# Where the experts end in a two-block transformer kernel: the fold of the experts' sum moves into the last down part, VectorE's usual way past the overflow test stands first and takes the norm in, SyncE loads the next projection's first slots inside its own branch

## The reference, cut to what matters

```python
def _moe(h, w_router, w_gate, w_up, w_down):            # layer 1 of the first block
    ...
    for e in range(N_EXPERTS):
        out = out + gates[..., e:e + 1] * _swiglu(h, w_gate[e], w_up[e], w_down[e])
    return out
...
    x = x + g2 * y                                      # g2 is a row over the 1024 columns
...
def second_block(x, norm1_g, w_in, ...):
    h = rms_norm(x, norm1_g[l])
    proj = h @ w_in[l]                                  # z, xbc, dt, q, k, v, two gates
    ...
    xbc = silu(causal_dwconv(xbc, conv_w, conv_b))      # 4 taps along the tokens
```

## Time and profile before

| | |
|---|---|
| median of 3 runs | 2148.12 us |
| the 3 runs | 2144.53, 2148.12, 2155.45 us |
| span of the profiled execution | 2154.6 us, mean TensorE clock 0.951 |
| time of the profiled execution | not told apart from the three; the longest, 2155.45, is 0.8 above the span |
| TensorE busy | 2001.1 us, 93% |
| VectorE busy | 1670.7 us, 78% |
| ScalarE busy | 1329.6 us, 62% |
| experts' last us and border | about 1330 to 1440 us of the span |

### The profile page before, as it was taken

How to read it: one execution, slowest core, us unless ns; L and a number is a source line. 1 busy time by engine, 2 the same in 40 slices (tenths; PEclk the granted TensorE clock), 3 DMA queues, 4 the chain that set the end, 5 groups by cost and what they waited for, 6 DMA issues and landing times. The chain is left out here.

```text
span 2154.6 us, 27980 instructions
## 1 busy us (share of the span) xinstructions
PE 2001.1 (93%) x11071; PEld 1718.9 (80%) x11071; DVE 1670.7 (78%) x2154; ACT 1329.6 (62%) x1969; POOL 0.2 (0%) x4
## 2 busy tenths in 40 slices
PE   7878999987899999999999999979999988889999
PEld 4668778877778888888888887769877877878997
DVE  5877888676679989998998999778665755567884
ACT  2654443366578777787877776657556644545662
POOL 0000000000000000000000000000000000000000
PEclk8977999998899999999999999999999999889999
DMA  7625688731259989998999998745414532224553
GB/s 297 227 80 194 262 317 329 265 142 40 98 194 370 366 335 358 361 363 327 362 361 347 344 374 319 271 179 177 137 59 139 196 132 99 81 90 148 193 177 117
DMA packets 70377, 497.18 MB, mean 231 GB/s; under 512 B 8032, under 2 KB 8288, under 8 KB 10976
## 3 DMA queue, kind: packets, MB, share of 16 engines
q1 hardware_dynamic: 69952, 494.28, 62.4%
q10 hardware_dynamic: 288, 1.05, 0.1%
HBM read 494.25 MB, written 1.05 MB: 230 GB/s over the span
## 5 line engine op out<-in xcount | busy, mean ns | idle before, releaser
L338 DVE TENSOR_TENSOR wlo<-ring,whi 128x1024 fp32r<-128x1024 f32 (+1 forms) x845 | 1016.3, 1216 | 283.3 <-ACT whi L384 265.4
L384 ACT ACTIVATE whi<-ring 128x1024 fp32r<-128x1024 f32 (+1 forms) x845 | 886.1, 1054 | 494.7 <-PE ps L236 447.5
L236 PE MATMUL ps<-whi,hT 128*128 128x256 f32 (+2 forms) x944 | 323.3, 343 | 26.9 <-DVE hTl L292 7.0
L236 PE MATMUL ps<-wlo,hT 128*128 128x256 f32 (+2 forms) x944 | 317.6, 336 | 0.0
L236 PE MATMUL ps<-whi,hTl 128*128 128x256 f32 (+2 forms) x944 | 317.0, 336 | 0.0
L236 PE MATMUL ps<-whi,xg 128*128 128x512 f32 (+1 forms) x768 | 290.6, 378 | 5.4 <-DVE wlo L338 5.2
L236 PE MATMUL ps<-whi,xgl 128*128 128x512 f32 (+1 forms) x768 | 286.8, 373 | 0.0
L236 PE MATMUL ps<-wlo,xg 128*128 128x512 f32 (+1 forms) x768 | 286.4, 373 | 0.0
L236 PEld LDWEIGHTS ps<-whi,hT 128*128 128x128 f32 x944 | 185.5, 196 | 51.4 <-issue 7.1
L236 PE MATMUL ps<-whi,hf 128*128 128x512 f32 x528 | 209.5, 397 | 6.5 <-DVE wlo L338 4.7
L236 PE MATMUL ps<-wlo,hf 128*128 128x512 f32 x528 | 206.9, 392 | 0.0
(11 more groups left out here) (286 smaller groups left out, 2628.5 us busy)
## 6 DMA issues: line engine op xcount, KB each, us to landing
ring<-in_wstream SPq DMA_DIRECT2D x462, 1024.0 KB, 5.1
ring<-in_wstream SPq DMA_DIRECT2D x4, 832.0 KB, 5.3
ring<-in_wstream SPq DMA_DIRECT2D x6, 256.0 KB, 2.7
cst<-in_cst SPq DMA_DIRECT2D x1, 1028.0 KB, 7.5
x<-in_x SPq DMA_DIRECT2D x1, 1024.0 KB, 13.6
work<-in_bias ACTq DMA_DIRECT2D x2, 512.0 KB, 5.2
ring<-in_wstream SPq DMA_DIRECT2D x2, 512.0 KB, 3.8
out_x<-x SPq DMA_DIRECT2D x1, 512.0 KB, 2.8
```

The costliest lines, as they stand in the source:

```text
L236: i = self.e.matmul(out, lhsT, rhs, start=start, stop=stop, skip_group_check=True)
L338: i = self.e.tensor_tensor(K.wlo[:, q % NS, 0:cols], src, hi.bitcast(F32), ALU.subtract)
L384: i = self.e.activation(K.whi[:, q % NS, 0:cols], K.ring[:, m % RING, at:at + cols], ACT.Copy)
```

## The change

It has four parts. (1) `dve_fold` leaves group 3 of gate and up and stands in expert 7's down part, a quarter behind the low halves of parts 6, 8, 10 and 12; the overflow test follows two chunks later. (2) VectorE no longer uses `when_over` but `when_few`: the test is turned round, the usual way (128 or fewer) falls through, and the second pass is the `Else`. Both ways now hold the norm n1 as well, with chunks 0 and 1 of xbc ahead of its blocks; the usual way ends with a jump past the second pass. (3) ScalarE makes the high halves of chunks 0 and 1 among the squares, BETWEEN leaves chunks 2 and 3 (before blocks 4 and 6), and TensorE spreads the root after 8 of the 16 transposes instead of after all. (4) SyncE loads the first four slots of xbc inside its branch; on the usual way it waits for the ring slots as the eight experts leave them (`earlier`), and not for the step.

```diff
@@ -368,7 +368,7 @@
                 i = self.e.activation(out, a, fn, scale=scale, bias=bias, accum_out=accum)
             i.then_inc(self.done.sem, inc)
 
-    def split_to(self, n):
+    def split_to(self, n, fence=None):
 
         K = self.K
         while self.q < n:
@@ -378,7 +378,7 @@
             cols = blocks[0][2] * len(blocks)
             self.wait_ge(K.full[m % RING], 16 * (m // RING + 1))
             if q >= NS:
-                self.wait_ge(K.pe, ("w", q - NS))
+                self.wait_ge(K.pe, ("w", q - NS if fence is None else earlier(q, fence, NS)))
             inc = K.hi.up()
             if self.e is not None:
                 i = self.e.activation(K.whi[:, q % NS, 0:cols], K.ring[:, m % RING, at:at + cols], ACT.Copy)
@@ -395,14 +395,14 @@
         super().__init__(K, e, K.sp, K.full)
         self.m = 0
 
-    def load_to(self, n):
+    def load_to(self, n, fence=None):
 
         K = self.K
         while self.m < n:
             m = self.m
             self.m += 1
             if m >= RING:
-                self.wait_ge(*K.last_use[m - RING])
+                self.wait_ge(*K.last_use[m - RING if fence is None else earlier(m, fence, RING)])
             full = K.full[m % RING]
             inc = full.up(by=16)
             if self.e is not None:
@@ -411,6 +411,48 @@
                 off = K.off[index]
                 src = K.wstream[off * 128:(off + cols) * 128].rearrange("(p c) -> p c", p=128)
                 self.e.dma_start(K.ring[:, m % RING, 0:cols], src).then_inc(full.sem, inc)
+
+
+def earlier(m, fence, ring):
+
+    return fence - 1 - (fence - 1 - m) % ring
+
+
+def when_few(K, x, body, first, then):
+
+    if x.e is None:
+        q, held = x.q, dict(x.held)
+        first()
+        head = [s.n for s in x.own]
+        body()
+        K.over = (head, [s.n for s in x.own], x.q)
+        then(True)
+        x.held = held
+        return
+    head, tail, behind = K.over
+    q, held, had = x.q, dict(x.held), [s.n for s in x.own]
+    v = x.e.value_load(K.count[0:1, 8:9], min_val=0, max_val=256)
+    with x.e.If(v <= 128):
+        first()
+        assert head == [s.n for s in x.own]
+        for s, n, m in zip(x.own, head, tail):
+            x.e.wait_ge(s.sem, n)
+            x.e.sem_inc(s.sem, m - n)
+            s.n = m
+        x.q = behind
+        then(False)
+        after, ended = x.q, [s.n for s in x.own]
+    with x.e.Else():
+        K.again = True
+        for s, n in zip(x.own, had):
+            s.n = n
+        x.q, x.held = q, dict(held)
+        first()
+        body()
+        then(True)
+        assert x.q == after and ended == [s.n for s in x.own]
+        K.again = False
+    x.held = held
 
 
 def when_over(K, x, body, first=None, then=None):
@@ -648,7 +690,8 @@
         for i in range(2):
             pe.wait_ge(K.dve, after_rows(s, p if len(halves) > 1 else 1, i, way))
         pe_turn(K, pe, s, lambda j, i: K.x[:, i, 128 * j:128 * j + 128], j1, "v", banks=banks, first=j0)
-    pe_along(K, pe, s)
+        if p == (0 if s == "n1" else len(halves) - 1):
+            pe_along(K, pe, s)
 
 
 def pe_along(K, pe, s):
@@ -718,7 +761,7 @@
 
 
 
-BETWEEN = {"nm0": ("inA0", {2: 2, 4: 3, 6: 4}), "nf0": ("ffng", {4: 3, 6: 4}), "nm1": ("inA1", {4: 3, 6: 4}), "n1": ("xbc", {2: 1, 4: 2, 6: 4}),
+BETWEEN = {"nm0": ("inA0", {2: 2, 4: 3, 6: 4}), "nf0": ("ffng", {4: 3, 6: 4}), "nm1": ("inA1", {4: 3, 6: 4}), "n1": ("xbc", {4: 3, 6: 4}),
            "n2": ("up2", {4: 3, 6: 4})}
 
 
@@ -1619,12 +1662,10 @@
         a.split_to(min(last + 1 + NS, K.fence(last)))
 
 
-def dve_gate_up(K, v, s, key, tiles, hf, at_part=None, at=0, later=None):
+def dve_gate_up(K, v, s, key, tiles, hf, at_part=None, at=0):
     for c, (n0, n, parts) in enumerate(groups(K, key + "g", KT)):
         if c == at and at_part is not None:
             at_part()
-        if c == 3 and later is not None:
-            later()
         v.split_to(min(parts[-1] + 1 + NS, K.fence(parts[-1])))
         if c:
             dve_turn_hidden(K, v, s, hf, c - 1, 512, tiles)
@@ -2020,17 +2061,15 @@
             for n in range(4):
                 v.split_to(first + 3 + n + NS - 1)
                 dve_add(K, v, last, e - 1, n, True)
-    def fold():
-        if e == NE - 1 and not over:
-            for n in range(4):
-                v.split_to(K.parts[key + "u"][8 + n] + NS - 1)
-                dve_fold(K, v, n)
-    dve_gate_up(K, v, s, key, 1, K.hf1, at_part=at_up, later=fold)
+    dve_gate_up(K, v, s, key, 1, K.hf1, at_part=at_up)
     parts = K.parts[key + "d"]
     v.split_to(parts[2] + NS - 1)
     dve_turn_hidden(K, v, s, K.hf1, 5, 256, 1)
     if e == NE - 1 and not over:
-        v.split_to(parts[9] + NS)
+        for n in range(4):
+            v.split_to(parts[4 + 2 * n] + NS - 1)
+            dve_fold(K, v, n)
+        v.split_to(parts[11] + NS)
         return
     if picks_next(e, over):
         v.split_to(parts[4] + NS - 1)
@@ -2077,9 +2116,12 @@
 
     def squares(way):
         by = ("x", 7) if way else ("e", 7)
+        xbc, fence = K.parts["xbc"][0], None if way else K.parts["moe7d"][-1] + 1
         act_squares(K, a, "n1", 0, 0, 512, lambda i: (by, "add", 2 * i))
         act_root_ahead(K, a)
+        a.split_to(xbc + 1, fence)
         act_last_squares(K, a, "n1", 512, lambda i: (by, "add", 2 * i + 1))
+        a.split_to(xbc + 2, fence)
     when_over(K, a, lambda: [over(e) for e in range(NE)], then=squares)
 
 
@@ -2106,7 +2148,13 @@
         dve_finish(K, v, s, K.parts[f"moe{e}xd"], False)
         for n in range(4):
             dve_add(K, v, s, e, n, False)
-    when_over(K, v, lambda: [over(e) for e in range(NE)], first=end)
+
+    def norm(way):
+        dve_eps(K, v, "n1")
+        dve_root(K, v, "n1")
+        v.split_to(K.parts["xbc"][0] + 2)
+        dve_mod_t(K, v, "n1", K.col("n1", 0, 8))
+    when_few(K, v, lambda: [over(e) for e in range(NE)], end, norm)
 
 
 def pe_cols(K, pe, key, n_blocks, last, block, banks=(0, 1, 2, 3), at_block=None):
@@ -2717,9 +2765,6 @@
             dve_dense(K, v)
         else:
             dve_moe(K, v)
-    dve_eps(K, v, "n1")
-    dve_root(K, v, "n1")
-    dve_mod_t(K, v, "n1", K.col("n1", 0, 8))
     barrier(K, v, ("ffn", 1))
     dve_ssd(K, v)
     barrier(K, v, "ssd")
@@ -2749,7 +2794,11 @@
     fences = K.slot_fences
     sp.load_to(fences[0])
     sp.wait_ge(K.dve, "most")
-    when_over(K, sp, lambda: sp.load_to(fences[1]))
+
+    def ahead(way):
+        sp.m = fences[1]
+        sp.load_to(fences[1] + RING, None if way else fences[0])
+    when_over(K, sp, lambda: sp.load_to(fences[1]), then=ahead)
     sp.load_to(len(K.slots))
     out = K.out_d.rearrange("(i p) d -> p i d", p=128)
     sp.wait_ge(K.dve, ("f2", "y", 1, 0))
```

## The result

The changed kernel takes 2138.95 us (median of four runs, 2133.02 to 2145.18) against 2151.78 us before (four runs, 2144.53 to 2159.73). The ratio is 0.993, 95% interval 0.990 to 0.996: 15 us less, between 9 and 21. The profiled execution's span went from 2154.6 to 2143.4 us, 11.2 less. One of the six runs of a kernel further down, the fold in groups 1 to 4, took 8357 us at a mean granted clock of 0.22 and is left out of its ratio.

What follows compares the result with a forecast made beforehand. TensorE, busy 93% of the span, bounds the kernel, plus its waits for VectorE's low halves. Terms -7.05 - 3.5 - 3.5 = -14.0 us, off the median 2148.1, give 2134.1 us; range 2127 to 2143.

Steps and rivals of the forecast that it cites:

- The fold leaves gate and up: Expert 7's gate and up: without the fold's pause and slow clock, it takes 7.05 us less.
- A: Distance from expert 6's last hf1l to expert 7's; forecast 95.8 us, 102.86 before.
- The fold enters the down part, the jump leaves the test: Expert 7's down part: three small stalls replace the 2.78 us pause, clock stays up; -3.5 us, bounds -5.6 and -0.7.
- B: Distance from expert 7's last hf1l to the first ffn_w of its product; 30.01 us before, 26.22 changed.
- The norm: Norm before xbc: chunks 0 and 1 lie ready, so chunk 4 starts 3.5 us sooner despite the moved jump.
- C: Distance from the first ffn_w of expert 7's product to TensorE's xbc chunk 4; 36.12 us before, 31.38 changed.
- the bound at -4.8: Lowest bound of the norm's gain, if VectorE's moved jump takes 2.7 us like ScalarE's.
- Two signs that I had named: Behind the norm: VectorE idle some 5 us after the last hTl; chunk 4 starting some 10 us after block 7.
- The clock did not fall in the small pauses: Rival: in the down part the clock falls in the fold's small stalls, losing 2.8 us; -11.2, 2137 us; 15%.
- The moved jump did not eat the gain: Rival: behind the norm a jump of 8.7 us cancels the norm's gain; -10.5, 2138 us; 12%.
- The rival of the cheap jump: Rival: the jump behind the norm is cheap and the folds are hidden; -17.5, 2131 us; 10%.
- the pause of 1.92 us: TensorE's pause where the last two low halves stand behind expert 7's product; forecast to stay, clock not lowered after it.

Runs made afterwards that it cites:

- the fold in groups 1 to 4: Changed kernel with one fold quarter at the start of each of gate and up's groups 1 to 4, chunk 0's low half before the root; ratio to before 0.992.
- Fold back: Changed kernel with all four quarters of the fold back in expert 7's gate and up in one piece; ratio to before 0.996.
- work behind the norm: Changed kernel with eight more VectorE operations (5.8 us, into an unread scratch tile) behind the end of its usual way; ratio to before 0.998.
- SyncE late: Changed kernel with SyncE's first four xbc slots loaded behind its branch, as before; ratio to before 0.9965.
- jump at the test: Changed kernel with VectorE's way past the test as before, the usual way reached by a taken jump there; ratio to before 0.993.
- only the fold moved: Kernel before with just the fold moved into expert 7's down part and the overflow test two chunks later; ratio to before 0.997.
- far apart: Changed kernel with fold quarters at the start of gate and up's groups 1, 3 and 5 and behind part 8 of the down part; ratio to before 0.993.

## Why the prediction was right, point by point

The forecast was 2134.1 us, 14.0 less; measured were 12.8 between the medians and 15 by the ratio, and the parts sum to 15.6. All three terms came out near their size; the share of the jump in the second, and its price in the third, did not.

- **The fold leaves gate and up**, -7.05: A fell by 7.08 (102.86 less 95.78). The like pair of experts was a good ruler. Fold back shows its fixed part, the pause of 4.08, and that the clock's part varies (A grew by 5.9 in that pair).
- **The fold enters the down part, the jump leaves the test**, -3.5: B fell by 3.79. Against the 24.05 us of a down part without pauses, the old jump had cost 5.96 (I had 2.78 and 2.8) and the three small pauses cost 2.2, where I had 2.0; the clock stayed up. The price of the test that falls through, nothing, is right. What I had wrong is the credit. I counted the old jump as a fixed 4.8; two kernels with the jump two chunks later lost only 1.2 and 1.5 us by it. So 2.3 of the 3.8 us come with the fold and the later test alone, since the jump there took 3.2 us and not 5.0, which I had not foreseen; turning the test round is worth 1.2 to 1.5.
- **The norm**, -3.5: C fell by 4.74. The first xbc matmul came 5.63 us sooner after eps, where I had 5.5. The term was mis-sized at the moved jump. It takes 2.9 us and not 4.8, and I had put it in a row behind VectorE's last hTl as if VectorE could go on at once without it. VectorE has to wait there for ScalarE's high half of chunk 4, 2.17 us with no jump at all; in the kernel before, 4.16 us. So the jump adds 0.44 us to VectorE's wait and nothing to TensorE's time, since chunk 0's bank is free 1.6 us before TensorE comes. That was the direction of the bound at -4.8. TensorE was paced by hT as assumed, 14.84 us up to chunk 4. Two signs that I had named failed with this: VectorE's idle time there is 2.6 us and not some 5, and chunk 4 starts 6.9 us after block 7 and not some 10 (my own times gave 7.8).
- **The rule of the Trainium skill** that a taken branch to a far target waits for the fetch (Runtime: NRT & Kernel Launch, Instruction fetch mechanics) agrees with every jump here; none took less than 2.4 us, and each of those timed in the last section holds a packet of the kind "instruction". It did not speak against the move in the end, since VectorE waits at the place behind the norm anyway. The 51 ns that the Trainium skill gives an unconditional branch (Advanced Engine Details and Errata, Control Flow Timing) fit the branch's own row (51 to 55 ns) and not what follows it.
- **The rivals.** The clock did not fall in the small pauses, in any of the five kernels that have them. The moved jump did not eat the gain. The rival of the cheap jump was half right: the jump was cheap, while the folds were not hidden.
- **Not foreseen** was that the clock at the pause of 1.92 us falls or stays up from trace to trace: it was low in five of ten, 1.6 to 2.0 us each; I had taken the one trace with 1.00 for the rule.

What stays open: why the clock falls behind the same pause in one trace and not in another, work behind the norm and the changed kernel being alike there. Early slots without the moved chunks, and the earlier spread of the root, have no run of their own. And turning the test round on TensorE, whose own jump delays the transposes by 2.4 to 3.0 us, was not tried.

## What to carry to other kernels

Where one engine runs a small lead ahead of the bound one (here 1.6 to 2.0 us: 5.7 us of fold gave pauses of 4.08 and 3.85, 4.77 us of idle time one of 2.78), extra work costs what exceeds the lead at once: put it in pieces shorter than the lead, and so far apart that the slack between them pays each back. A jump past rarely used code costs microseconds on whichever side it lies; put it where its own engine waits for another anyway and the bound engine has work in hand, and do not price it by one trace. When work is moved ahead of a critical step, its loads must be moved with it, or they stop what is queued behind.

## What the runs showed of the hardware

The time of a taken jump varies with the moment at which one small DMA packet runs. Lines 481 and 498 of ScalarE (branch, then the first semaphore step), in the changed kernel and with SyncE late, where no ring load runs there:

```profile
L481 ACTq COMPARE_BRANCH  x1: 50/50/50, 1390.7 to 1390.7; - x1
...
L498 ACTq EVENT_SEMAPHORE  x2: 17/17/17, 1396.3 to 1396.4; - x2
```

```profile
L481 ACTq COMPARE_BRANCH  x1: 50/50/50, 1387.4 to 1387.4; - x1
...
L498 ACTq EVENT_SEMAPHORE  x2: 17/17/17, 1389.9 to 1390.0; - x2
```

It is 5.6 us with the ring being filled and 2.5 without, for the same jump. The ten traces agree: in the seven with early slots, where the DMA engines are 0.95 busy or more during ScalarE's jump, it takes 5.0 to 5.9 us; in the three without, at a DMA share of 0.01, 2.5 to 2.7.

The DMA view lists the packets by kind, and in each of these ten stretches there is exactly one of the kind "instruction". In 0.1 us windows it is found at 1394.6 in the changed kernel and at 1388.3 with SyncE late:

```profile
q14 instruction: 1, 0.01, 19.3%
```

```profile
q14 instruction: 1, 0.01, 29.6%
```

| jump | from the branch to this packet, us | from the packet to the next work, us |
|---|---|---|
| ScalarE, no ring loads (3 traces) | 0.9 to 1.1 | 1.6 to 1.8 |
| ScalarE, among ring loads (7 traces) | 3.3 to 4.2 | 1.6 to 1.7 |
| VectorE at the test, kernel before | 3.2 | 1.8 |
| VectorE at the test, jump at the test | 1.0 | 1.8 |
| VectorE at the test, only the fold moved | 1.0 | 2.2 |
| VectorE behind the norm, work behind the norm | 1.0 | 1.9 |

So nearly all of the difference lies ahead of the packet, and the rest is nearly fixed. That the packet belongs to the jump, and that it queues behind the ring's packets, is inferred: it fits ScalarE's ten traces. It is not a rule that loads make a jump long: VectorE's at the test had its packet after 1.0 us at DMA shares of 0.87 and 0.79, and after 3.2 us at 0.58. Why it came late there is open. SyncE's jump took 4.5 to 4.8 us in seven traces, and 6.1, 6.3 and 6.8 in the other three (the fold in groups 1 to 4, far apart, SyncE late).
